# Latent attention's scores as two passes of 128 rows and one of 32, with the rotary rows of four banks on four row groups

## What is computed

```
q = (rms_norm(cq) @ w_qb)      # per head 64 plain + 32 rotary columns
kv = (rms_norm(ckv) @ w_kvb)   # per head 64 of k, 64 of v
q_rope, k_rope = rotate(...)   # k_rope is one for all heads
logits = (q_nope.k_nope + q_rope.k_rope) * 96 ** -0.5
probs = softmax(logits); o = probs @ v
y = (o * silu(z)) @ w_out
```

## Time and profile before

| | us |
|---|---|
| median of three runs | 2940.75 |
| the profiled execution | 2935.45 |
| its span | 2934.1 |
| TensorE busy in the span | 2789.7 (95%) |
| VectorE, ScalarE, GpSimd | 1594.6, 1351.5, 849.5 |
| first score matmul to the last Exp of the stage | 537.1 (787.86 to 1324.98) |
| granted TensorE clock, mean | 0.984 |

### The profile page before, as it was taken

One profiled execution on the slowest core, in us unless ns is written; L12 is line 12 of the kernel. 1 busy time (PEld: TensorE's weight loads), 2 busy tenths in 40 slices (PEclk: granted clock), 3 DMA queues, 4 the chain that ended last, 5 costly groups with the idle time before them and its releaser, 6 DMA issues.

```text
span 2934.1 us, 36292 instructions
## 1 busy us (share of the span) xinstructions
PE 2789.7 (95%) x13800; PEld 2277.5 (78%) x13800; DVE 1594.6 (54%) x2767; ACT 1351.5 (46%) x2482; POOL 849.5 (29%) x669
## 2 busy tenths in 40 slices
PE   8999999998899999999996999999999999999997
PEld 6878777776788888887774777778787888887875
DVE  6667774633388888887467665532002444433034
ACT  5668854334366666674434334541113333333122
POOL 0334441223344445542121221123221111112331
PEclk9999999999999999999998999999999999999999
DMA  3101141211100000004111110032211001001231
GB/s 130 40 29 41 40 140 54 94 65 36 33 10 10 10 10 10 17 23 144 44 58 73 48 36 22 22 100 84 68 44 43 23 29 36 23 29 48 75 115 72
DMA packets 54443, 148.77 MB, mean 51 GB/s; under 512 B 6144, under 2 KB 14976, under 8 KB 54272
## 3 DMA queue, kind: packets, MB, share of 16 engines
q1 hardware_dynamic: 54272, 146.46, 15.4%
HBM read 129.66 MB, written 16.78 MB: 50 GB/s over the span
## 4 chain that ended last, share of the span: by engine, by line
PE 84%; DVE 7%; ACT 5%; issue 3%; POOL 1%; DMA 0%; ACTq 0%; DVEq 0%; POOLq 0%
PE ps L327 78%; PE ps L417 4%; ACT t L311 1%; PE ps L2515 1%; PE ps L740 1%; DVE t L1604 0%; ACT t L779 0%; DVE t L1894 0%; DVE t L870 0%; DVE t L1786 0%; DVE t L2861 0%; DVE t L839 0%; DVE t L1777 0%; POOL t L318 0%; DVE t L1790 0%
## 5 line engine op out<-in xcount | busy, mean ns | idle before, releaser
L327 PE MATMUL ps<-t,t 128*128 128x512 f32 (+5 forms) x11912 | 2625.6, 379 | 113.2 <-issue 12.8
L327 PEld LDWEIGHTS ps<-t,t 128*128 128x128 f32 (+2 forms) x11912 | 2075.5, 185 | 592.8 <-issue 113.5
L318 POOL TENSOR_TENSOR t<-t,t 128x1024 fp32r<-128x1024 f32 (+2 forms) x169 | 355.1, 2102 | 1286.9 <-ACT t L311 1286.4
L311 ACT ACTIVATE t<-t 128x1024 fp32r<-128x1024 f32 (+2 forms) x205 | 187.0, 912 | 651.5 <-PE ps L327 651.4
L1660 POOL TENSOR_SCALAR t<-t,t 128x1024 f32<-128x1024 f32 x128 | 145.5, 1137 | 182.9 <-DVE t L1610 179.9
L1604 DVE TENSOR_TENSOR t<-ps,t 128x512 fp32r<-128x512 f32 x256 | 164.3, 682 | 15.7 <-ACT t L1521 13.9
L417 PE MATMUL ps<-t,t 128*128 128x128 f32 x1176 | 160.5, 274 | 12.8 <-DVE t L1604 7.6
L417 PEld LDWEIGHTS ps<-t,t 128*128 128x128 f32 x1176 | 131.8, 141 | 36.8 <-issue 25.0
L1617 DVE TENSOR_REDUCE t<-ps 128x1 f32<-128x1024 f32 x128 | 154.1, 1204 | 1.8 <-PE ps L327 1.8
L1521 ACT ACTIVATE t<-ps 128x512 fp32r<-128x512 f32 x256 | 140.2, 591 | 11.3 <-PE ps L417 7.2
L1529 ACT ACTIVATE t<-ps,t 128x1024 f32<-128x1024 f32 x128 | 142.9, 1117 | 1.9 <-DVE t L1617 1.5
(11 more groups left out here) (223 smaller groups left out, 2426.6 us busy)
## 6 DMA issues: line engine op xcount, KB each, us to landing
t<-in_wflat SPq DMA_DIRECT2D x156, 512.0 KB, 3.6
t<-in_wada SPq DMA_DIRECT2D x48, 256.0 KB, 4.3
t<-in_xT SPq DMA_DIRECT2D x16, 512.0 KB, 6.9
t<-in_wflat SPq DMA_DIRECT2D x32, 128.0 KB, 2.0
hd<-t SPq DMA_DIRECT2D x8, 512.0 KB, 3.0
t<-hd SPq DMA_DIRECT2D x8, 512.0 KB, 7.2
x2d<-t SPq DMA_DIRECT2D x8, 512.0 KB, 2.6
md<-t SPq DMA_DIRECT2D x16, 256.0 KB, 4.3
```

The costliest lines, as they stand in the source:

```text
L311: ac.activation(parts(i)[0][:, 0:n], raw[i % 2][:, 0:n], ACT.Copy).then_inc(*on.up(ac, "whi", i))
L318: e.tensor_tensor(lo[:, 0:n], raw[i % 2][:, 0:n], hi[:, 0:n], ALU.subtract) \
L327: return pe.matmul(o, l, r, start=start, stop=stop)
```

## The change

- Q and K tiles get 128 used rows in two passes. Pass 0: rows 0-63 high q by high k, rows 64-127 the rotary part (q high and q low rows against k high twice). Pass 1: rows 0-63 low q by high k, rows 64-127 high q by low k. The product left, rotary q high by rotary k low, is a matmul of 32 rows: tiles `QR` and `KR` hold it four times, in row groups 0, 32, 64 and 96, one for each of banks 0 to 3.
- `scores(p)` handles two blocks at once, in even steps: eight matmuls of 128 rows, then four of 32 rows, one per row group and bank.
- Rows move between partitions by DMAs from SBUF to SBUF on SP's queue: seven kinds x0 to x6 of 32 or 64 rows by 512 columns; at most one of a kind is in flight. For each half of q: six; for each half of k: one. For k's rotary rows: six per half, once.
- `QR` lies in the upper halves of the weight buffers (high and low), which narrow weights of the stage leave free; so the first two blocks of the output projection are split only in step 128 (`i == NI`), after the last scores.
- VectorE takes the maxima of both blocks in the even step; `head_dv` runs one step later (i - 1 in head_step), after the output sum and before `pair_dv`. The gate product moves from VectorE to GpSimd, right after the scaling. ScalarE does the Exp before the turned copies.

```
+        KR = at(YO + 57344, [P, T], F32R)
+        QR = [[at(WO + 4096 * (2 * s + hf) + 2048, [P, H], F32R) for hf in range(2)] for s in range(2)]
+        def copy(x, key, to, src):
+            if x in in_flight:
+                on.wait_ge(sp, *in_flight[x])
+            in_flight[x] = (f"x{x}/d", *key)
+            sp.dma_start(to.bitcast(F32), src.bitcast(F32)).then_inc(*on.landed(sp, f"x{x}/d", *key))
...
 def rope_users(h, hf):
-    users.append((("b", h, hf), ("roped", "q", h, hf, 0)))
+    users.append((("b", h, hf), ("x4/d", "q", h, hf)))
...
 def tensor(): ...
-        if i < NI:
-            scores(i)
+        if i < NI and i % 2 == 0:
+            scores(i // 2)
...
+def scores(p):
+    h, b = divmod(2 * p, 8)
+    s, hf = h % 2, b // 4
+    on.wait_ge(pe, "q_lo", h, hf)
+    on.wait_ge(pe, "k_lo", h, 1)
+    for x in range(6):
+        on.wait_ge(pe, f"x{x}/d", "q", h, hf)
+    on.wait_ge(pe, "x6/d", "q", h, 1)
+    for w in range(2):
+        qs = slice((b + w) * P, (b + w) * P + P)
+        for y in range(2):
+            for c in range(2):
+                if y == 0:
+                    wait_bank(2 * w + c)
+                mm(ps[:, 2 * w + c, :], Qs[s][y][:, qs], Ks[s][y][:, half(c)], y == 0, False)
+                freed[2 * w + c] = [("b exp", 2 * p + w)]
+    for w in range(2):
+        qs = slice((b + w) % 4 * P, (b + w) % 4 * P + P)
+        for c in range(2):
+            r = slice(64 * w + 32 * c, 64 * w + 32 * c + 32)
+            t = mm(ps[:, 2 * w + c, :], QR[s][hf][r, qs], KR[r, half(c)], False, True)
+        t.then_inc(*on.up(pe, "b scores", 2 * p + w))
...
 def scalar(): ...            # the turned copies (L1515 to L1521) now stand below the Exp
+        if i == NI:
+            on.wait_ge(ac, "b scores", NI - 1)
+            w_hi(BO)
+            w_hi(BO + 1)
...
 def vector(): ...
-        if i < NI: ... max of i
+        if i < NI and i % 2 == 0:
+            block_max(i)
+            block_max(i + 1)
         if i >= 5 and i % 2: ... sum of the output halves
-            dv.tensor_tensor(g, t, g, ALU.mult).then_inc(*on.up(dv, "b og", p))
+        if i - 1 in head_step:
+            head_dv(*head_step[i - 1])
         if i in pair_step:
             pair_dv(*pair_step[i])
-        if i in head_step:
-            head_dv(*head_step[i])
...
 def gpsimd(): ...
             po.tensor_scalar(Pm[u][:, :], ...)                        # scaling of block i - 1
+        if i >= 5 and i % 2:
+            on.settled(po)
+            on.wait_ge(po, "b sum", p)
+            po.tensor_tensor(OG[vr, h // 2, qs], T_["o", p][0][vr, 0:256], OG[vr, h // 2, qs], ALU.mult)
+            on.settled(po)
+        if i == NI:
+            w_lo(po, BO)
+            w_lo(po, BO + 1)
         if i in head_step:
             head_po(*head_step[i])                                    # unchanged
...
 def sync(): ...              # behind the three w_load ahead of the loop
+    for s in range(4):
+        head_copies(0, s)
     for i in range(NI + 4):
         if i in head_step:
+            head_copies(h, s)
+def head_copies(h, s):
+    hf, c, x = s % 2, half(s % 2), h % 2
+    if s < 2:
+        on.wait_ge(sp, "q_hi", h, hf)
+        copy(5, ("q", h, hf), Qs[x][1][64:128, c], Qs[x][0][0:64, c])
+        on.wait_ge(sp, "roped", "q", h, hf, 2)
+        for n, r in enumerate((0, 32, 96)):
+            copy(n, ("q", h, hf), QR[x][hf][r:r + 32, :], QR[x][hf][64:96, :])
+        copy(3, ("q", h, hf), Qs[x][0][64:96, c], QR[x][hf][64:96, :])
+        copy(4, ("q", h, hf), Qs[x][0][96:128, c], T_["b", h, hf][0][64:96])
+    else:
+        on.wait_ge(sp, "k_hi", h, hf)
+        copy(6, ("q", h, hf), Ks[x][1][0:64, c], Ks[x][0][0:64, c])
```

More of the change, by code:

```diff
@@ L1218, in program, with key_copies @@
         ktab = Y([P, T])
+        KR = at(YO + 57344, [P, T], F32R)
+        QR = [[at(WO + 4096 * (2 * s + hf) + 2048, [P, H], F32R) for hf in range(2)] for s in range(2)]
+        in_flight = {}
+        def copy(x, key, to, src):
[3 more added lines that the diff above has]
+            sp.dma_start(to.bitcast(F32), src.bitcast(F32)).then_inc(*on.landed(sp, f"x{x}/d", *key))
+        def key_copies(hf):
+            c = half(hf)
+            on.wait_ge(sp, "roped", "k", hf, 2)
+            copy(0, ("k", hf), Ks[0][0][96:128, c], Ks[0][0][64:96, c])
+            copy(1, ("k", hf), Ks[1][0][64:96, c], Ks[0][0][64:96, c])
+            copy(2, ("k", hf), Ks[1][0][96:128, c], Ks[0][0][64:96, c])
+            copy(3, ("k", hf), KR[0:32, c], KR[64:96, c])
+            copy(4, ("k", hf), KR[32:64, c], KR[64:96, c])
+            copy(5, ("k", hf), KR[96:128, c], KR[64:96, c])
         Pm = [Y([P, T]), Y([P, T])]
@@ L1375, in gpsimd @@
                         w_lo(po, LR + 2)
[L1376 to L1381, removed]
+                    rope_gpsimd(T_r["a", hf][0], T_r["b", hf][0], Ks[0][0][64:96, half(hf)], KR[64:96, half(hf)], ("k", hf))
                 for i in Z:
@@ L1391, in sync @@
                     w_load(i + 4)
+                    if i in Z[2:4]:
+                        key_copies(i - Z[2])
             tensor()
@@ L1405, in stage_attn_b @@
             HQ, HK, HV = BLK["hq"], BLK["hk"], BLK["hv"]
+            BO = BLK["bo"][0]
             T_ = {}
@@ L1410, in stage_attn_b, with small @@
             pair_step = {16 * r + x: (r + 1, s) for r in range(B_HEADS // 2 - 1) for s, x in enumerate((15, 17, 19, 20))}
+            def small(split, i):
+                if i < BO:
+                    split(i)
             def order_of_users():
@@ L1469, in pair @@
                     freed[b] = [("b v_hi", r, c), ("b v_lo", r, c)]
[L1471 to L1478, removed]
-                on.wait_ge(pe, "k_lo", h, 1)
[L1480 to L1483, removed]
+            def scores(p):
+                h, b = divmod(2 * p, 8)
+                s, hf = h % 2, b // 4
+                on.wait_ge(pe, "q_lo", h, hf)
+                on.wait_ge(pe, "k_lo", h, 1)
+                for x in range(6):
+                    on.wait_ge(pe, f"x{x}/d", "q", h, hf)
[14 more added lines that the diff above has]
+                    t.then_inc(*on.up(pe, "b scores", 2 * p + w))
             def turn_p(i):
@@ L1514, in scalar @@
                 for i in range(NI + 4):
[L1515 to L1521, removed]
                     if 1 <= i < NI + 1:
@@ L1529, in scalar @@
                         ac.activation(Pm[u][:, :], o, ACT.Exp, bias=bm[:, c0:c0 + 1], accum_out=bm[:, c0 + 1:c0 + 2]).then_inc(*on.up(ac, "b exp", i - 1))
+                    if i == NI:
+                        on.wait_ge(ac, "b scores", NI - 1)
+                        w_hi(BO)
+                        w_hi(BO + 1)
+                    if 3 <= i < NI + 3:
+                        for c in range(2):
+                            on.wait_ge(ac, "b pT", i - 3, c)
+                            to, src = turned(i - 3, c, 0)
+                            if i - 3 >= 4:
+                                on.wait_ge(ac, "b out", (i - 3) // 2 - 2)
+                            ac.activation(to, src, ACT.Copy).then_inc(*on.up(ac, "b pT_hi", i - 3, c))
                     if i >= 5 and i % 2:
@@ L1649, in head_dv @@
                     on.wait_ge(dv, "k_hi", h, hf)
-                    dv.tensor_tensor(Ks[h % 2][1][0:64, half(hf)], src, Ks[h % 2][0][0:64, half(hf)], ALU.subtract).then_inc(*on.up(dv, "k_lo", h, hf))
+                    dv.tensor_tensor(Ks[h % 2][1][64:128, half(hf)], src, Ks[h % 2][0][0:64, half(hf)], ALU.subtract).then_inc(*on.up(dv, "k_lo", h, hf))
             def gpsimd():
@@ L1670, in head_po @@
                     if hf:
-                        w_lo(po, HQ[h] + 2)
+                        small(lambda n: w_lo(po, n), HQ[h] + 2)
                     for ev in slot_free(h):
                         on.wait_ge(po, *ev)
-                    rope_gpsimd(T_["a", h, hf][0], T_["b", h, hf][0], *(t[64:96, half(hf)] for t in Qs[h % 2]), ("q", h, hf))
+                    rope_gpsimd(T_["a", h, hf][0], T_["b", h, hf][0], QR[h % 2][hf][64:96, :], T_["b", h, hf][0][64:96].bitcast(F32R), ("q", h, hf))
                 elif hf and h % 2 == 0:
-                    w_lo(po, HK[h // 2] + 2)
+                    small(lambda n: w_lo(po, n), HK[h // 2] + 2)
             def sync():
```

50 lines of the change are left out of this document (29 added, 21 removed).

## The result

The changed kernel takes 3142.52 us, the kernel before on the same chip 2940.61: ratio 1.0687 [1.0655, 1.0720], slower by 202 us. The forecast was 3073 with a range of 2998 to 3115: right in sign, too small by a third, and the time lies outside the range.

A forecast was written before the change was run, and what follows sets the result against it. TensorE bounds the kernel before; afterwards a loop through VectorE and GpSimd would. Heads and light pairs +123.4, start +12.6, last head -3.6, end +4.5: +137 on 2935.45, 3072, stated as 3073 us; range 2998 to 3115.

The forecast's parts named there:

- The moved step: VectorE's rope products of a new head, one step later behind the output sum: stretches the attention loop, +123 us with its waits.
- The loop through GpSimd: Closed chain from turn to turn through output sum, rope and GpSimd's scaling: 10.9 us, twice a head, 21.9 us.
- just covered: Copy that frees an output's temporary: issues and landing take 2.5 to 4.4 us, needed about 4.4 us after the rope.
- the one bank: Bank 7, shared by the loop's projections: q frees it 2 us or more later, so v projection, v transposes and scores wait.
- the sum of two heads, 84.5: Step-by-step layout of an even and an odd head, 42.0 and 42.5 us: 84.5 us instead of 68.3.
- the short pass: Four 32-row matmuls of a pair's scores: 0.45 us, making a pair 2.15 us, 0.4 saved.
- Rival 4: TensorE's clock falls after idle gaps in the loop: 1.7 us lost at each of 30, +51, 3123 us; chance 0.12.
- Rival 3: The four short matmuls don't run together: 0.85 us or more instead of 0.45, +24, 3096 us; chance 0.14.
- that rule: A tiling-mode change drains TensorE: 0.25 us twice a pair would make a pair 2.65 us, with nothing saved.
- Start: First scores wait for 14 copies on SP behind the weight loads: at 800.5 instead of 787.86, +12.6 us.
- Light pairs: Pairs without projection, held by both Exps and maxima: 7.1 us each; last head 28.9 to its last Exp, -3.6.
- the end: Late output-weight splits before the last turned copies and outputs: 13.4 us instead of 8.86, +4.5.

The follow-up runs named there:

- p1_rope_late: The kernel before with one move alone: VectorE makes the next head's low parts and rope products in step i+1, behind the output sum; 3142.51 us, ratio 1.0690.
- x1_dv_back: The changed kernel with VectorE's next-head step (`head_dv`) put back in step i, behind `pair_dv`; 3011.65 us, ratio 1.0258 to the kernel before.
- x2_po_late: The changed kernel with GpSimd too taking up the rope one step later, behind the scaling and the output product; 3135.47 us, ratio 1.0670 to the kernel before.
- c1_filler: The changed kernel with throwaway matmuls in TensorE's idle gaps, ahead of v projections, v transposes and odd heads' first two turns; 3116.02 us, ratio 1.0596.
- x7_full_third: The changed kernel with VectorE's step back in step i and four 128-row matmuls (a wrong product) for the short ones; 3026.06 us, ratio 1.0291.

## Why the prediction was off

- **The moved step costs most: right.** That VectorE's step, not the scores, decides, holds in both directions (`p1_rope_late` +202, `x1_dv_back` -126 to -131). The costs don't add: 202 and 74 separately, 202 together. The likely reason, which no run shows by itself, is that the pairs' waits fall into the time that TensorE waits anyway.
- **The loop through GpSimd: right in the odd heads, wrong in the even ones.** The forecast had it close twice in every head, some 30 times; TensorE's turn waited for the scaling 16 times, 35.6 us. In the odd head turn to turn is 10.87 us (10.9 forecast; its links as listed add up to 11.1). There the copy that frees the output's temporary, "just covered" in the forecast, ended last 6 times, 10.3 us in all, and the chain of waits of `x2_po_late` leads through it. In the even head what the forecast called **the one bank** carries it, then `v_lo` and `k_lo`. That a second link of nearly the same length stood beside the scaling is the likely reason that `x2_po_late` wins nothing; no run cuts both.
- **The step that failed is the sum of two heads, 84.5.** One repeat took 91.8 and the mean 92.6, so it was too small by 7.3 to 8.1, and fifteen heads came out 61.7 us too short. The path was near enough; three terms on it were put at nothing or mis-sized. The clock had no term in the sum: behind the gaps eight score loads took 2.38 and 3.02 instead of 1.69, a v projection's six 2.21 instead of 1.23, together 3.0 us in one even head; `c1_filler`, with the clock back, has two heads in 89.1 and the whole time 27 us less. The values' wait for `v_lo` (1.67 at 1212.54) was not laid out. And the short pass: 0.45 was its load time alone; with 0.36 us idle before and 0.24 behind it takes 0.79, and 8 full loads with it 2.48 (1233.11 to 1235.59) instead of 2.15, eight times in two heads: 2.6. The three add up to about 7.3. Only the clock's part has a run of its own.
- **Rival 4 was true beside the forecast, not instead of it.** It had 1.7 us a gap on 30 gaps; the rows behind the three gaps of two heads show 0.7, 1.3 and 1.0, so 3.0 in two heads. Behind the gap before 1188.04 the granted clock was 0.59 in 1188 to 1192 (near the lower of its two levels, 1.2 GHz), and 1.00 (2.4 GHz) again in 1230 to 1236. With gaps of 3.7 to 4.1 us, 15 to 16 us apart, the mean clock in 1000 to 1200 was 0.93; in `x1_dv_back`, whose longest gap there is 1.8 us, it was 1.00. The Trainium skill, "TensorE: Matmul & The Clock Gate", section "HAM oscillation — how this bites in real kernels", tells of short bursts between waits for DMAs; here the bursts stand between waits for VectorE, and the trace shows the same sign (2.21 us instead of 1.23 for six loads behind a gap).
- **Rival 3: false,** with the run of one row group as evidence. But the drain that the Trainium skill names ("TensorEngine Tiling (Array Packing)", section "Key Properties") agrees with the trace, and it takes most of the saving back: 0.60 us of idle time for each of 64 passes, none around the twelve full loads of `x7_full_third`. The forecast had weighed that rule with 0.25 us twice, 2.65 us a pair, and did not take it; measured is 2.48.
- **Start: 20.9 instead of 12.6.** SP's copies in the changed kernel (start, us from first to last issue, count) and one DMA group (count, KB, landing):

```profile
796.45 40.84 SPq L1234 DMA_DIRECT2D t<-t  x26
...
t<-t SPq DMA_DIRECT2D x160, 64.0 KB, 2.0
t<-t SPq DMA_DIRECT2D x64, 128.0 KB, 2.3
```

  The landing was as forecast (2.0); the issue of a copy took 0.58 in the median, above my 0.1 to 0.48, on 14 copies in a row. The wait for the last copy is 19.60 us, where TensorE waited 2.10 before. The other 3.4 of the 20.9 are not the copies': the matmuls ahead ended that much later, and in `p1_rope_late`, which has no copies, the first score comes 2.7 us late too.
- **Light pairs and the end: near.** The last head has 7.4 a pair (7.1 forecast), and 31.3 us to its last Exp (28.9); its first eight score loads took 3.06 us at the low clock. The end is 14.09 (13.4).
- **The base of the sum.** The forecast added its 137 us to the profiled execution, 2935.45; added to the median 2940.75 it would have been 3078, not 3073. That changes nothing above.
- **The range** took its high end from one rival alone. Several small misses of one sign (clock, `v_lo`, drain, start) lie on the same chain and add up.

## What to carry to other kernels

When a step moves to a later place in an engine's order, draw the loop through every buffer that it frees, a shared PSUM bank first, and give each loop its own price. The longest decides, and it can be another one from head to head: here bank 7 in the even heads, GpSimd's scaling or the landing of a copy in the odd ones. An experiment that cuts one of two equal loops shows no gain, and that is no proof that the loop isn't there. Packing short matmuls into row groups is worth the matmuls it saves less two drains, and less whatever the pairing does to the engines behind; measure the pairing alone before building the layout. Where a layout has gaps as long as those here (3.7 to 4.1 us), put the cost of the clock into the sum and not into a rival.

## What the runs showed of the hardware

- A group of four 32-row matmuls amid 128-row ones leaves 0.36 us idle ahead of its loads and 0.24 behind when the four are in four row groups, 0.36 on both sides when they are in one.
- TensorE at 78% busy, but with gaps of 3.7 to 4.1 us, had a mean clock of 0.93; `c1_filler`, with matmuls whose result nobody reads in the gaps, had 1.00 in 1000 to 1200 and was 27 us faster.
- A copy from SBUF to SBUF of 64 or 128 KB lands in 2.0 to 2.3 us in the median, but its issue on SP takes 0.58; by that, as an estimate, 14 in a row are over 8 us ahead of whoever waits for the last.
